# A hybrid decoder step: the first weight block and the tokens in one table loaded in three parts, constants later, the fourth projection block on raw tokens

## The reference, cut to what matters

```python
def rmsnorm(x, g):
    y = xf * lax.rsqrt(jnp.mean(xf * xf, axis=-1, keepdims=True) + EPS)
    return (y * g.astype(jnp.float32)).astype(x.dtype)

h = rmsnorm(xp, norm_mix[l])
xr, q, k, v, g_rnn, g_attn = split_in(h, w_in[l])      # z = h @ w_in, D_MODEL 1024
conv_in = jnp.pad(xr, ((0, 0), (CONV_W - 1, 0), (0, 0)))
y_rnn, h_last = rg_lru(causal_conv(conv_in, conv_w[l], conv_b[l]), ...)
...                                   # windowed attention, gates, output projection
...                                   # top-4-of-32 experts: w_up (32,1024,2048), w_down (32,1024,1024)
```

## Time and profile before

| | |
|---|---|
| device time, median of 3 runs | 1148.07 us (1147.60 to 1148.33) |
| span of the profiled execution | 1146.0 us |
| PE busy | 1113.5 us (97%) |
| DVE, ACT, POOL busy | 311.8, 229.6, 34.0 us |
| read from memory | 436.00 MB, 383 GB/s over the span |
| chain that ended last | PE 69%, DMA 24%, DVE 3%, ACT 2% |

### The profile page before, as it was taken

One profiled execution on the slowest core, in us unless ns is written; L12 is line 12 of the kernel. 1 busy time (PEld: TensorE's weight loads), 2 busy tenths in 40 slices (PEclk: granted clock), 3 DMA queues, 4 the chain that ended last, 5 costly groups with the idle time before them and its releaser, 6 DMA issues.

```text
span 1146.0 us, 14903 instructions
## 1 busy us (share of the span) xinstructions
PE 1113.5 (97%) x5772; PEld 493.6 (43%) x5772; DVE 311.8 (27%) x785; ACT 229.6 (20%) x642; POOL 34.0 (3%) x69
## 2 busy tenths in 40 slices
PE   8999999999999999999999999999999999999997
PEld 6687778844333424333333333323232323232432
DVE  5665544032131221212130312121213030312123
ACT  4564363422020202010101111111111101010103
POOL 0200012210000000000000000000000000000000
PEclk9999999999999999999999999999999999999999
DMA  9743636989999999999999999999999999999995
GB/s 350 265 153 111 187 112 265 426 350 421 427 428 426 426 427 428 428 428 428 427 428 428 430 429 428 427 428 429 429 429 427 427 428 429 429 427 427 426 427 238
DMA packets 40802, 437.90 MB, mean 382 GB/s; under 512 B 6720, under 2 KB 9040, under 8 KB 11072
## 3 DMA queue, kind: packets, MB, share of 16 engines
q1 hardware_dynamic: 40136, 435.65, 91.2%
q10 hardware_dynamic: 624, 1.68, 0.4%
HBM read 436.00 MB, written 2.41 MB: 383 GB/s over the span
## 4 chain that ended last, share of the span: by engine, by line
PE 69%; DMA 24%; DVE 3%; ACT 2%; issue 1%; DVEq 0%; SPq 0%; ACTq 0%
PE bank L1319 21%; DMA ring<-in_w_down 20%; PE bank L1355 19%; PE bank L1055 8%; PE bank L1100 5%; PE bank L1201 4%; DMA area<-in_w_down 3%; PE bank L1222 3%; PE bank L1150 2%; PE bank L1235 1%; PE bank L1198 1%; PE bank L1036 1%; PE bank L1225 1%; DVE area L1748 1%; PE bank L923 1%
## 5 line engine op out<-in xcount | busy, mean ns | idle before, releaser
L1319 PE MATMUL bank<-ring,area 128*64 128x512 f32 x1744 | 396.4, 597 | 9.1 <-DMA ring<-in_w_up 8.7
L1319 PEld LDWEIGHTS bank<-ring,area 128*64 128x64 f32 x1744 | 117.2, 136 | 261.8 <-issue 222.9
L1355 PE MATMUL bank<-ring,area 128*64 128x512 f32 x928 | 213.7, 599 | 7.5 <-DMA ring<-in_w_down 7.5
L1736 DVE TENSOR_TENSOR x_tok<-x_tok,bank 128x512 f32<-128x512 f32 x60 | 41.3, 688 | 328.0 <-PE bank L1222 328.0
L800 ACT ACTIVATE area<-area 128x256 f32<-128x256 f32 x64 | 26.7, 417 | 516.3 <-DVE area L1748 516.3
L1055 PE MATMUL bank<-ring 128*128 128x264 f32 (+1 forms) x512 | 121.7, 393 | 0.0
L1355 PEld LDWEIGHTS bank<-ring,area 128*64 128x64 f32 x928 | 62.4, 136 | 117.9 <-issue 102.7
L1055 PEld LDWEIGHTS bank<-ring 128*128 128x128 f32 x512 | 95.2, 190 | 21.3 <-issue 4.0
L1773 DVE TENSOR_TENSOR area<-area 128x1024 f32<-128x1024 f32 x15 | 18.4, 1225 | 211.3 <-ACT area L810 211.3
L1222 PE MATMUL bank<-area 128*128 128x512 f32 x128 | 71.8, 644 | 0.0
L1319 PE MATMUL bank<-area 128*64 128x512 f32 x304 | 69.2, 597 | 1.5 <-DMA area<-in_w_up 1.5
(11 more groups left out here) (271 smaller groups left out, 702.6 us busy)
## 6 DMA issues: line engine op xcount, KB each, us to landing
ring<-in_w_up SPq DMA_DIRECT2D x103, 2048.0 KB, 34.3
ring<-in_w_down SPq DMA_DIRECT2D x51, 2048.0 KB, 33.9
area<-in_w_up SPq DMA_DIRECT2D x17, 2048.0 KB, 29.8
ring<-in_w_in SPq DMA_DIRECT2D x16, 1024.0 KB, 9.3
ring<-in_w_down SPq DMA_DIRECT2D x13, 1024.0 KB, 10.6
ring<-in_w_up SPq DMA_DIRECT2D x12, 1024.0 KB, 9.7
area<-in_w_down SPq DMA_DIRECT2D x5, 2048.0 KB, 34.3
ring<-in_w_out SPq DMA_DIRECT2D x8, 1024.0 KB, 5.0
```

What stands on the lines that cost most here:

```text
L1319: m = mm(bank[2 * h + n][64 * e:64 * e + 64, :], xe[:, k, 64 * e:64 * e + 64], w[:, kk, e, NB * n:NB * (n + 1)], start=False, stop=(k == K ...
L1355: m = mm(bank[4 + c][64 * e:64 * e + 64, :], y_t[:, 4 * half + f, 64 * e:64 * e + 64], w[:, f, e, :], start=False, stop=(half == 1 and f = ...
L1736: eng.tensor_tensor(x, x, combined_bank(unit, last)[:, :], ALU.add).then_inc(s.added, 1)
```

## The change

- `in_opening` is a new table with one row for each partition: 8 norm weights, then for each piece 256 weights of the first block and 280 token values. SP loads it in three parts, before anything else: 1080, 1072 and 2144 words of each row (553, 549 and 1098 KB). `vec` comes fourth, and block 1 fifth. The first block has left the ring of slots; the slots of all other blocks are the same.
- ACT issues the load of `keep` behind `x_scale(0)`. It squares pieces 6 and 7 as well (L624). DVE squares only 4 and 5, adds in steps of two pieces, and does the three small softplus steps between them instead of first.
- PE runs 12 matmuls of `keep_warm` and not 14. `norm_sum` stands behind the first piece of block 2 instead of before the last piece of blocks 0 and 1. Block 3 works on `xn`, as block 2 does, and `after_kv` comes behind block 3. `h_t` is first needed by block 4.
- DVE scales block 3 too (`raw_block(1)`, behind the convolution of piece 0); before, ACT copied it out.
- One memset of POOL waits for `sum_done`, since the table now lies over its target.

```diff
@@ sync @@
-            eng.dma_start(vec[:, :], vec_cols).then_inc(s.rows_loaded, 16)
-            head = blocks[:, trunk_slot(0), :]
-            for part, sem in enumerate((s.head_loaded0, s.head_loaded1)):
-                c, k = slice(2 * COLS * part, 2 * COLS * (part + 1)), slice(2 * part, 2 * part + 2)
-                eng.dma_start(head[:, c], w_in[0][:, c]).then_inc(sem, 16)
-                eng.dma_start(x_raw[:, k, :], x_cols[:, k, :]).then_inc(sem, 16)
-            eng.dma_start(x_raw[:, KB // 2:, :], x_cols[:, KB // 2:, :]).then_inc(s.xr_loaded, 16)
-            eng.dma_start(head[:, 4 * COLS:], w_in[0][:, 4 * COLS:]).then_inc(block_full[trunk_slot(0)], 16)
+            ends = (0, *(KB + k * (COLS + T) for k in (2, 4, KB)))
+            for part, sem in enumerate(open_loaded):
+                c = slice(ends[part], ends[part + 1])
+                eng.dma_start(opened[:, c], opening[:, c]).then_inc(sem, 16)
+            eng.dma_start(vec[:, :], vec_cols).then_inc(s.rows_loaded, 16)
@@ gpsimd @@
-            eng.memset(q_t[:, :, 0:N_META], 0.0).then_inc(s.zeroed, 1)
...
+            eng.wait_ge(s.sum_done, 1)
+            eng.memset(q_t[:, :, 0:N_META], 0.0).then_inc(s.q_zeroed, 1)
@@ scalar @@
+            eng.wait_ge(s.open_loaded0, 16)
+            x_scale(0)
             eng.dma_start(keep[:, :], c_in[:, 0:C_KEEP]).then_inc(s.consts_loaded, 16)
...
+            eng.wait_ge(s.open_loaded1, 16)
+            x_scale(2)
+            act(sq[:, 0:KB // 2, :], x_raw[:, 0:KB // 2, :], ACT.Square).then_inc(s.sq_done, 1)
+            eng.wait_ge(s.open_loaded2, 16)
+            for k in range(KB // 2, KB):
+                x_scale(k)
+                if k == KB - 3:
+                    act(sq[:, KB - 2:KB, :], x_raw[:, KB - 2:KB, :], ACT.Square).then_inc(s.sq_done, 1)
@@ tensor @@
-            keep_warm(14, bank[7])
+            keep_warm(12, bank[7])
...
-                if k == KB - 2:
-                    norm_sum()
...
                 for k in range(KB):
-                    if n == 3 and k % 2 == 0:
+                    if n == 2 and k == 1:
+                        norm_sum()
+                    elif n == 4 and k % 2 == 0:
                         eng.wait_ge(s.h_ready, k // 2 + 1)
                     m = mm(proj_bank(n)[:, 0:T - lo], w[:, k, P * (n % 2):P * (n % 2) + P],
-                           (xn if n == 2 else h_t)[:, k, lo:T], start=(k == 0), stop=(k == KB - 1))
+                           (xn if n < 4 else h_t)[:, k, lo:T], start=(k == 0), stop=(k == KB - 1))
                 m.then_inc(s.proj_done, 1)
-                {2: after_kv, 4: keys_major}.get(n, lambda: None)()
+                {3: after_kv, 4: keys_major}.get(n, lambda: None)()
@@ vector @@
+            eng.wait_ge(s.sq_done, 1)
+            eng.tensor_tensor(sq[:, 0:2, :], sq[:, 0:2, :], sq[:, 2:4, :], ALU.add).then_inc(s.sq_add, 1)
+            eng.wait_ge(s.open_loaded2, 16)
+            eng.tensor_tensor(sq[:, 4:6, :], x_raw[:, 4:6, :], x_raw[:, 4:6, :], ALU.mult).then_inc(s.sq_own, 1)
...
                 if j == 0:
+                    raw_block(1)
                     token_major()
```

More of the change, by code:

```diff
@@ L71 @@
 ATT = BLK_Q + 5
+OPENING = KB + KB * (COLS + T)
 BEHIND = (-1, 14, 4, 4, 4, 4, 4, 4)
@@ L340, in program @@
         a_t, b_t, g_r, q_t = (up(KB) for _ in range(4))
-        x_raw, xn, sq, kv_t, tanh_t = a_t, b_t, xc, g_r[:, 0:2, :], g_r
+        xn, sq, kv_t, tanh_t = b_t, xc, g_r[:, 0:2, :], g_r
+        open_at = pair_at + 2 * KB * T
+        opened = upper[:, open_at:open_at + OPENING]
+        norm_w = opened[:, 0:KB]
+        body = opened[:, KB:OPENING].rearrange("p (k c) -> p k c", k=KB)
+        w_first, x_raw = body[:, :, 0:COLS], body[:, :, COLS:COLS + T]
         bias_in = upper[0:3 * E_N, pair_at:pair_at + 3 * D]
@@ L1406, in stepper @@
                 return step
+            for part in range(2):
+                k = 2 * part + 1
+                eng.wait_ge(open_loaded[part], 16)
+                eng.tensor_scalar(xn[:, k, :], x_raw[:, k, :], norm_w[:, k:k + 1], None, ALU.mult)\
+                   .then_inc(s.xn_v, 1)
+            eng.wait_ge(s.sq_done, 1)
+            eng.tensor_tensor(sq[:, 0:2, :], sq[:, 0:2, :], sq[:, 2:4, :], ALU.add).then_inc(s.sq_add, 1)
+            eng.wait_ge(s.open_loaded2, 16)
+            eng.tensor_tensor(sq[:, 4:6, :], x_raw[:, 4:6, :], x_raw[:, 4:6, :], ALU.mult).then_inc(s.sq_own, 1)
+            eng.wait_ge(s.sq_add, 1)
+            eng.wait_ge(s.sq_own, 1)
+            eng.tensor_tensor(sq[:, 0:2, :], sq[:, 0:2, :], sq[:, 4:6, :], ALU.add).then_inc(s.sq_add, 1)
             eng.wait_ge(s.rows_loaded, 16)
@@ L1414, in _ @@
             sp(eng.tensor_copy(sm[:, 0:8], v[1]))
-            for part, sem in enumerate((s.head_loaded0, s.head_loaded1)):
-                k = 2 * part + 1
-                eng.wait_ge(sem, 32)
-                eng.tensor_scalar(xn[:, k, :], x_raw[:, k, :], vec[:, NRM + k:NRM + k + 1], None, ALU.mult)\
-                   .then_inc(s.xn_v, 1)
-            eng.wait_ge(s.xr_loaded, 16)
-            hi = slice(KB // 2, KB)
-            eng.tensor_tensor(sq[:, hi, :], x_raw[:, hi, :], x_raw[:, hi, :], ALU.mult).then_inc(s.sq_done, 1)
-            eng.wait_ge(s.sq_done, 2)
-            for step, n in enumerate((KB // 2, KB // 4)):
-                if step:
-                    eng.wait_ge(s.sq_add, step)
-                eng.tensor_tensor(sq[:, 0:n, :], sq[:, 0:n, :], sq[:, n:2 * n, :], ALU.add).then_inc(s.sq_add, 1)
-            eng.wait_ge(s.sq_add, 2)
+            eng.wait_ge(s.sq_add, 2)
+            eng.wait_ge(s.sq_done, 2)
+            eng.tensor_tensor(sq[:, 0:2, :], sq[:, 0:2, :], sq[:, 6:8, :], ALU.add).then_inc(s.sq_add, 1)
+            eng.wait_ge(s.sq_add, 3)
             eng.tensor_tensor(ssum, sq[:, 0, :], sq[:, 1, :], ALU.add).then_inc(s.sq_add, 1)
@@ L1926 @@
     arrays["in_x_cols"] = np.ascontiguousarray(columns(tokens))
+    first = inputs["w_in"][0][:, W_IN_ORDER[0]:W_IN_ORDER[0] + COLS].reshape(KB, P, COLS).transpose(1, 0, 2)
+    body = np.concatenate([first, columns(tokens)], axis=2).reshape(P, KB * (COLS + T))
+    arrays["in_opening"] = np.ascontiguousarray(np.concatenate([inputs["norm_mix"][0].reshape(KB, P).T, body], axis=1))
     arrays["in_conv_states"] = np.ascontiguousarray(columns(inputs["state_conv"][0].reshape(B_S * PAD, D)))
```

87 lines of the change are left out of this document (40 added, 47 removed).

## The result

The changed kernel takes **1156.68 us** (median of 4, 1155.81 to 1158.28) beside 1147.84 us of the kernel before in the same session (median of 4, 1146.85 to 1148.33). The ratio is 1.008, 95% interval 1.0068 to 1.0093. So it is 0.8% slower, where 1147.7 with a range of 1146.5 to 1149.0 had been forecast. The profiled execution has a span of 1154.4 us, 8.4 more than before.

The account below looks back on a forecast made before the run. The weights' stream, tied to PE, was taken to bound the kernel; `norm_sum` at 14.17 instead of 14.54 gains 0.37 us at no cost, giving span 1145.6 and, with 2.07 us to the median, 1147.7 us, range 1146.5 to 1149.0.

Parts of the forecast that it names:

- no hindrance: PE's opening: the 12 warm-up matmuls end at 5.07 us, ahead of the first matmul at 5.76, so they don't delay it.
- What bounds the kernel: Late experts: the weights' stream is slower than PE but tied to it, so opening shifts reach the end one for one.
- The arrival of the data: Opening loads: the table's first part lands at 5.0 us and its third at 9.0.
- the term of 0.8 us for `keep`: Opening loads: taking the `keep` load from ahead of the table's parts lands the first and third 0.8 us earlier.
- PE's row of work: PE's opening blocks: first matmul at 5.76 us, `norm_sum` at 14.15 to 14.2 instead of 14.54.
- The new wait: PE ahead of `gates(0)`: a wait of some 1.2 us opens, since the chain from `norm_sum` keeps its 9.77 us.
- given away: PE's opening: moving `norm_sum` behind three more matmuls loses 1.47 us of the 2.0 us lead at the first matmul.
- Early landing: Rival, opening loads: parts land at 4.5 and 8.3 us as on a free queue; gain 0.9 us, 1147.1 us; 13%.
- The whole lead: Rival, `gates(0)`: no wait opens, so the first matmul's lead of 2.0 to 2.5 us counts; 1145.6 to 1146.1 us; 4%.
- Late landing: Rival, opening loads: cold start keeps loads slow, third part lands later, up to 2.0 us slower, 1150.1 us; 14%.
- Nothing reaches the end: Rival, after the opening: the shift is lost in a later wait on a load; 1148.1 us; 5%.
- The clock: Rival, PE's opening: fewer warm-ups or the wait before `gates(0)` drop the clock to half; +3.9 us, 1152.0 us; 2%.

Follow-up runs that it names:

- the pair further on: The kernel before with 251 and with 256 more instructions of repeated waits ahead of PE's expert loop: 1157.10 and 1148.07 us.
- the run with twenty instructions: The changed kernel with twenty more instructions of repeated waits ahead of PE's expert loop: 1146.91 us in one execution.
- the padded kernel: The changed kernel with five more instructions of repeated waits ahead of PE's expert loop: 1147.31 us, ratio 0.9996 to the kernel before.

## Why the prediction was wrong, step by step

**The step that failed** is in its first paragraph: "A moment that PE gains or loses in the opening moves the first expert load, and with it the end, by the same moment; it can't be multiplied. Hence the question is only when the opening lets PE go on." That took for granted that the opening reaches the rest only through time. It also reaches it through the length of PE's program. The edit that was costed at "no hindrance", two warm-up matmuls fewer, took four instructions from ahead of the loop, the change as a whole five, and that was worth 9 us and more (1156.7 and 1147.3 with five more, 1157.1 and 1148.1 in the pair further on), since the loop stood at the first of its 25 good places. None of the rivals named it, and the range had no room for it. What could have been read beforehand: the loop's begin and length in the two built programs, and that the queue of instructions brought 28 packets, of which one came in three turns.

That a moment is carried on one for one did hold where the loop was kept, up to the first jump: 0.61 us at `gates(0)` are 0.62 at 508, and 2.33 are 2.34. At the end they are 0.4 (interval -0.7 to 1.5) and 1.7 us (0.7 to 2.8), which is in keeping with it but doesn't show it: in between, where PE waits for the stream, the two leads of the profiled executions grew to 1.1 and 3.3 us in the middle of the last pair (1116.46 and 1114.21 instead of 1117.54).

**What bounds the kernel.** Right for the kernel before, and it hides part of the loss. A stall of PE is paid first from what the stream leaves it, 21.4 us from the second jump on.

**The arrival of the data.** DVE's and ACT's timelines of the changed kernel:

```profile
8.76 0.74 DVE L1424 TENSOR_TENSOR ring<-ring 128x560 f32<-128x560 f32 x1 [0.39 <-DMA ring<-in_opening]
...
11.65 0.45 DVE L1439 TENSOR_TENSOR area<-ring 128x280 f32<-128x280 f32 x1
```
```profile
4.75 0.53 ACT L612 ACTIVATE ring<-ring 128x280 f32<-128x280 f32 x1 [2.51 <-DMA ring<-in_opening]
```

First part 4.75 (forecast 5.0), third 8.76 (9.0), sum ready 12.10 (12.5). But the term of 0.8 us for `keep` was wrong. It costs nothing at the first part and 0.2 at the third. So the sum of the first part came out near only by luck, because another term was too small; whether that is the packet size (1.66 us) or the lag that was taken over from the trace of before was not tried apart.

**PE's row of work.** First matmul 5.53 (5.76), `norm_sum` 13.75 (14.15 to 14.2). Right in the main: 0.23 us of the difference are the earlier start, and the row up to `norm_sum` took 8.22 us instead of 8.35. "No hindrance" for the warm-up was not quite so. It had been counted to end at 5.07 and ran to 5.69, so the first matmul came 0.78 us behind the data instead of 0.68 as before; in the run with twenty instructions it came 1.4 us behind them.

**The new wait.** 1.42 us (1.2) on DVE's last convolution step; `gates(0)` 23.54 (23.9); from `norm_sum` to `gates(0)` 9.79 us (9.77). Right, and the run with `norm_sum` put back shows it once more: 21.98 - 12.19 = 9.79. There 1.72 us come back at `gates(0)` beside the padded kernel, where 1.47 had been called given away.

**`raw_block(1)`** cost nothing: from `gates(0)` to `gates(2)` 10.13 us, before 10.14.

**The rivals.** Early landing: nearest to what the opening did (gain 0.77, forecast 0.9), though the parts landed between the two forecasts, 4.75 (4.5 and 5.0) and 8.76 (8.3 and 9.0). The whole lead: no, the wait at `gates(0)` opened. Late landing: no. Nothing reaches the end: not in the kernel with `norm_sum` back, whose 1.7 us are clear of noise; the 0.4 us of the padded kernel are not. The clock: it fell, but in the experts, behind holes that the instruction fetch made; in the opening only in the kernel before with 12 warm-ups, where the block took 1.6 us longer (3.9 had been counted for it).

## What to carry to other kernels

Where an engine's program has a loop of nearly as many instructions as stay with it, count them, and look where the loop begins: any edit ahead of it, however harmless, may decide whether the loop is fetched once or in every turn. The profile shows it in two rows, the packets of the instruction queue and "issue" at the loop's first line; read them before you look for a cause in what was edited, and pad the program to the middle of the window when you compare two versions. And a large stall can hide behind slack: here 31 us of PE's time showed as 9.

## What the runs showed of the hardware

- A jump back to a packet that was not kept costs 3.5 to 3.8 us with one packet missing, 7.5 to 8.7 us with two, all of it in stretches where the weights keep the DMA engines full (share 1.00 to 1.02); no run shows it on idle ones. A loop that lies in seven packets of 256 instructions was kept through four turns in all of seven kernels.
- Behind the pairs of holes of the changed kernel PE's clock was granted at 0.50 for the first 3.4 to 6.2 us of work, worth 1.8 to 3.2 us each time. Behind a single hole of 3.47 us (the kernel before with 40 instructions more) it was still 1.00 as PE went on and fell to 0.50 within the next microsecond.
- Repeated waits that are already met are nearly free beside matmuls: 256 instructions of them cost some 0.5 us in 1148, which is within the spread of single executions.
- Behind twelve warm-up matmuls and a hole of 1.99 us the clock fell to 0.50, behind fourteen and 2.23 us it did not, in one execution each. The warm-up itself varied between executions: 12 matmuls took 4.2 to 5.3 us.
